# Streaming every second block backwards, and shifting where the weights lie in their slots

## The reference

```python
h = rms_norm(x, norm_g); proj = h @ w_in          # 2048 x 16512
...                                               # band attention, RWKV-7 scan, memory attention
merged = (sigmoid(ga) * (ya @ w_up_a) + sigmoid(gb) * (yb @ w_up_b) + sigmoid(gc) * (yc @ w_up_c))
x = x + merged @ w_o
...                                               # second layer: attention, gated linear attention, convolution
x = x + (silu(h2 @ w_ffn_gate) * (h2 @ w_ffn_up)) @ w_ffn_down
```

## Time and profile before

| | |
|---|---|
| median of 2 runs | 2914.97 us (2914.79 to 2915.15) |
| span of the profiled execution | 2913.4 us |
| PE busy | 2882.6 us, 99% |
| PE weight loads | 2491.1 us, 86%, beside the matmuls |
| DVE busy | 1619.3 us, 56% |
| ACT busy | 1344.1 us, 46% |
| HBM traffic | 177 GB/s over the span |

### The profile page before, as it was taken

How to read it: one execution, slowest core, us unless ns; L and a number is a source line. 1 busy time by engine, 2 the same in 40 slices (tenths; PEclk the granted TensorE clock), 3 DMA queues, 4 the chain that set the end, 5 groups by cost and what they waited for, 6 DMA issues and landing times.

```text
span 2913.4 us, 42709 instructions
## 1 busy us (share of the span) xinstructions
PE 2882.6 (99%) x18228; PEld 2491.1 (86%) x18228; DVE 1619.3 (56%) x1860; ACT 1344.1 (46%) x1533; POOL 73.7 (3%) x173
## 2 busy tenths in 40 slices
PE   7999999999999999999999999999999999999998
PEld 7979888888988888889998899888888888888886
DVE  5565665656656556564555466554654544544444
ACT  5452543544554454454455454444444444444443
POOL 5000000001000000000000000000000000000000
PEclk9999999999999999999999999999999999999999
DMA  7443444566665655566556566666566666666564
GB/s 211 125 143 112 134 128 118 166 195 184 227 194 184 189 163 185 191 188 182 174 161 202 166 174 174 196 194 195 192 184 195 188 193 188 188 189 206 192 194 152
DMA packets 356178, 518.30 MB, mean 178 GB/s; under 512 B 18288, under 2 KB 137220, under 8 KB 355220
## 3 DMA queue, kind: packets, MB, share of 16 engines
q1 hardware_dynamic: 355220, 512.37, 58.7%
q0 software_dynamic: 768, 3.20, 0.4%
HBM read 513.39 MB, written 2.11 MB: 177 GB/s over the span
## 4 chain that ended last, share of the span: by engine, by line
PE 98%; DVE 1%; ACT 0%; DMA 0%; issue 0%; SPq 0%; DVEq 0%; ACTq 0%
PE gp L1668 23%; PE gp L1670 23%; PE gp L1669 23%; PE gp L1677 7%; PE gp L1679 7%; PE gp L1678 7%; PE ps L1845 4%; PE ps L1727 1%; PE ps L1802 1%; PE ps L1833 1%; DMA gain<-in_norm_g 0%; PE ps L1787 0%; PE ps L1823 0%; PE ps L2045 0%; PE ps L2062 0%; PE ps L2053 0%
## 5 line engine op out<-in xcount | busy, mean ns | idle before, releaser
L1058 DVE TENSOR_TENSOR w_lo<-w_raw,w_hi 128x1024 fp32r<-128x1024 f32 (+2 forms) x976 | 1166.2, 1202 | 949.6 <-ACT w_hi L653 944.7
L653 ACT ACTIVATE w_hi<-w_raw 128x1024 fp32r<-128x1024 f32 (+2 forms) x976 | 1011.0, 1041 | 1106.4 <-PE gp L1670 877.7
L1668 PE MATMUL gp<-w_hi,h_hi 128*128 128x512 f32 x2112 | 833.5, 395 | 1.5 <-DVE w_lo L1058 1.5
L1670 PE MATMUL gp<-w_lo,h_hi 128*128 128x512 f32 x2112 | 822.7, 390 | 0.0
L1669 PE MATMUL gp<-w_hi,h_lo 128*128 128x512 f32 x2112 | 822.2, 389 | 0.0
L1677 PE MATMUL gp<-h_hi,w_hi 128*128 128x256 f32 x1696 | 488.4, 288 | 1.8 <-DVE h_lo L1123 1.8
L1678 PE MATMUL gp<-h_lo,w_hi 128*128 128x256 f32 x1696 | 474.5, 280 | 0.0
L1679 PE MATMUL gp<-h_hi,w_lo 128*128 128x256 f32 x1696 | 474.3, 280 | 0.0
L1668 PEld LDWEIGHTS gp<-w_hi,h_hi 128*128 128x128 f32 x2112 | 396.6, 188 | 83.8 <-DVE w_lo L1058 1.9
L1670 PEld LDWEIGHTS gp<-w_lo,h_hi 128*128 128x128 f32 x2112 | 396.5, 188 | 83.3
L1669 PEld LDWEIGHTS gp<-w_hi,h_lo 128*128 128x128 f32 x2112 | 396.8, 188 | 80.5 <-issue 0.5
(11 more groups left out here) (290 smaller groups left out, 1805.3 us busy)
## 6 DMA issues: line engine op xcount, KB each, us to landing
w_raw<-in_w_in SPq DMA_DIRECT2D x384, 512.0 KB, 4.0
w_raw<-in_w_ffn_gate SPq DMA_DIRECT2D x88, 512.0 KB, 4.4
w_raw<-in_w_ffn_up SPq DMA_DIRECT2D x88, 512.0 KB, 4.4
w_raw<-in_w_ffn_down SPq DMA_DIRECT2D x88, 512.0 KB, 4.1
w_raw<-in_w_in SPq DMA_DIRECT2D x136, 256.0 KB, 3.2
w_raw<-in_w_in SPq DMA_DIRECT2D x128, 192.0 KB, 3.1
w_raw<-in_w_mem_kv SPq DMA_DIRECT2D x32, 512.0 KB, 4.3
w_raw<-in_w_o SPq DMA_DIRECT2D x32, 512.0 KB, 4.3
```

Source lines behind the costliest of these rows:

```text
L653: act.activation(in_slot(w_hi, n), w_raw[:, slot, 0:size], ACT.Copy).then_inc(sem("hi_done"), 1)
L1058: dve.tensor_tensor(in_slot(w_lo, n), w_raw[:, slot, 0:size], in_slot(w_hi, n).bitcast(F32), ALU.subtract)\
L1668: pe.matmul(o, xh, wh, start=(k == 0), stop=False)
L1670: ins = pe.matmul(o, xh, wl, start=False, stop=(k == last_k))
```

## The change

The kind of block no longer decides alone where a unit lies. The blocks of each form are counted in pairs. Both of a pair get the same place in the slot: words 0, 63, 62, 61, 1, 2, 3 in turn for rows blocks, words 16, 0, 48, 32 for column blocks. The second of each pair is streamed backwards: its moving operand is read, and its PSUM output written, from the last column to the first. The sums are the same, column by column. The stationary operand is read forwards as before. Nothing else differs: instructions, their order, their waits and the DMAs are the same in number.

```diff
-SHIFT = {'rows': 0, 'wide': 16, 'pair': 16, 'trio': 16, 'narrow': 16}
+ROW_PLACES = (0, 63, 62, 61, 1, 2, 3)
+COLUMN_PLACES = (16, 0, 48, 32)
@@ build
+    place, back, of_form = [], [], Counter()
+    for b in blocks:
+        form = "rows" if b.kind == "rows" else "columns"
+        places = ROW_PLACES if form == "rows" else COLUMN_PLACES
+        place.append(places[of_form[form] // 2 % len(places)])
+        back.append(of_form[form] % 2 == 1)
+        of_form[form] += 1
...
+        def streamed(v, m):
+            return v[:, ::-1] if back[m] else v
...
         def in_slot(w, n):
-            at = SHIFT[blocks[units[n][0]].kind]
+            at = place[units[n][0]]
             return w[:, n % RING, at:at + unit_size(n)]
@@ PE's unit
-                        wh, wl = (in_slot(w, n)[:, j * 512:(j + 1) * 512] for w in (w_hi, w_lo))
+                        wh, wl = (streamed(in_slot(w, n)[:, j * 512:(j + 1) * 512], m) for w in (w_hi, w_lo))
...
-                            o = gp[:, s, a * 512:(a + 1) * 512]
+                            o = streamed(gp[:, s, a * 512:(a + 1) * 512], m)
...
-                        o = gp[:, s, c * T:(c + 1) * T]
+                        o = streamed(gp[:, s, c * T:(c + 1) * T], m)
+                        xh, xl = streamed(x_hi[k], m), streamed(x_lo[k], m)
...
-                        pe.matmul(o, wh, x_hi[k], start=(k == 0 and c % 2 == 0), stop=False, skip_group_check=True)
-                        pe.matmul(o, wh, x_lo[k], start=False, stop=False, skip_group_check=True)
-                        ins = pe.matmul(o, wl, x_hi[k], start=False, stop=(k == last_k), skip_group_check=True)
+                        pe.matmul(o, wh, xh, start=(k == 0 and c % 2 == 0), stop=False, skip_group_check=True)
+                        pe.matmul(o, wh, xl, start=False, stop=False, skip_group_check=True)
+                        ins = pe.matmul(o, wl, xh, start=False, stop=(k == last_k), skip_group_check=True)
```

## The result

The changed kernel takes 2983.72 us (median of 2 runs, 2982.74 to 2984.70) against 2914.97 us: 1.024 times as long, with a 95% interval from 1.021 to 1.027. The span of its profiled execution is 2983.0 us against 2913.4.

A forecast was written before the change was run, and what follows sets the result against it. PE's matmul pitches were taken to bound the kernel. 2913.4 + 3.2 (shifted start) + 0 + 0 gave a span of 2916.6 us; with 1.6 us between span and median, 2918 us; range 2844 to 3045 us.

The forecast's parts named there:

- rival 5: Address and direction don't touch PE's matmul pitch: 2915 us; chance 0.60, shared with the forecast itself.
- rival 3: Backward streams on PE pay one further cycle in 16 columns, 18 for 16: +71 us, 2989 us; chance 0.13.
- What bounds the kernel: PE, busy 2882.6 of 2913.4 us, hardly waits; the time is the sum of its matmuls' pitches.
- the counts: Rows blocks have 8928 matmuls, 7632 not at word 0, 4080 backwards; column blocks have 5088, 2544 backwards.
- The shifted start: Streamed weights of rows blocks starting off word 0: 0.42 ns a matmul, 3.2 us; ends 0 and 54 us.
- The backward stream: Reversed reading and PSUM writing in every second block on PE: taken as 0; ends -71 and +1223 us.
- POOL's row: POOL's reversed copy, 256 columns in 407 ns against 512 forward in 710, read as showing no backward penalty.
- Half rate backwards: Backward read or PSUM write on PE goes one column in two cycles: +1223 us, 4141 us; chance 0.17.
- Odd words straddle: Odd starts of PE's streams break every aligned pair of words fetched: +1132 us, about 4050 us; chance 0.03.
- The surplus goes in backward streams: PE's surplus cycle in 16 columns vanishes when streaming backwards: -71 us, 2847 us; chance 0.07.
- Column places: Stationary operand's words 16, 0, 48, 32 in column blocks: taken as 0; ends -13 and +9 us.
- Plain fp32: Score matmuls on PE read as 2.03 cycles a column without surplus, so the surplus belongs to fp32r operands.

## Why the prediction was right or wrong

The time, 2984 us, lies inside the range of 2844 to 3045 us, on the side "slower" that had a chance of 0.33; the likeliest value, 2918 us, which had 0.60 together with "nothing at all happens" (rival 5), was wrong by 66 us, and the result lies outside its own range of 2902 to 2973 us. That rival 3 came within 5 us, at 2989, is luck: it had 71 us from the direction and next to nothing from the places, where the direction alone cost 30.4 us and the places alone 47.3.

*What bounds the kernel* was right: PE's pitches alone carry the result, no wait of PE changed, and ACT and DVE stayed hidden. So were the counts, which turn the pitches into the 69 us. DVE's wait for ACT, which I had expected to stay near 945 us, rose to 1000.0, in step with PE's 70.4 us.

*The shifted start* is the step that failed first. I took 0.42 ns a matmul and 3.2 us in all; the places alone made the rows blocks 40.3 us longer, 5.3 ns for each of 7632 matmuls. The end of 54 us held, but I chose by DVE's two equal rows. DVE takes words at less than half the rate (1224 ns for 1024 of them against 0.443 ns each), and in plain fp32, at 429.2 ns a record, PE doesn't feel the address either. The row was near in form and says nothing of an fp32r stream. The surplus in the earlier trace rows had pointed the right way, and I used it only for the size of the smallest step.

*The backward stream* was taken at 0; alone it made the rows blocks 26.1 us longer, 6.7 ns for a backward matmul in most blocks. Rival 3 had the mechanism's form (a further share of a cycle for 16 columns of a backward stream) at twice the size: half a cycle more, not one, at place 0, and the full one only at places 3 and 63. POOL's row had the same fault as DVE's.

*Half rate backwards* (rival 1) didn't come, and neither side of its argument was needed: PSUM takes a step of -1 at no cost, against the rule that the Trainium skill gives in PSUM — Partial Sum Buffer, Specifications, if -1 is read as non-contiguous. For SBUF, the Trainium skill (SBUF — State Buffer, Specifications) asks for two hits in a line of 16 bytes for full bandwidth, and says too that each crossing to a new line pays a penalty. A step of 2 makes two hits and took 451.3 ns, so here the measurement decides against the two hits. My reading of the same row, that a backward unit step with its four hits changes nothing, was wrong by 6.7 ns at the least. *Odd words straddle* (rival 2) is refuted by words 7, 15, 39 and 63. *The surplus goes in backward streams* (rival 4) fell: 233.3 ns, not 213.

*Column places* were taken at 0 with +9 us as the upper end, on the ground that place 16 alone shows both pitches. The places alone cost 4.6 us (6.9 without the first block), the whole change 10.8 us there, with lasting pitches of up to 120 ns that the trace of before doesn't have. That end was too low: two observed pitches are not a bound.

*Plain fp32* was misread: the four records of the earlier trace rows are two matmuls, not four, so that a column costs four cycles and not two. Nothing in the sum hung on it, but a "half rate" was named after it.

What stays open is the rule. Shown is that at place 0 the cost of the direction arises in reading the moving operand from SBUF, that neither it nor place 1 costs anything in plain fp32, that the stationary operand's address and length take part, and that a pitch once taken holds on until a new block or other work comes: within a stretch of 60 or more matmuls of one block, the mean of 24 pitches moves by more than 1 ns in none of eleven traces. That the places cost by the same reading is argued: the shift alters nothing else of PE, and the pitch doesn't follow ACT's and DVE's work. What order of accesses makes 0, 7, 15, 39 and 63 free and 1, 5 and 17 dear was not found. That the places 61, 60 or 5 have two pitches each, in blocks of the same form, says that how the two streams begin relative to each other matters as well; this is argued, not shown.

## What to carry to other kernels

Where an engine's stream has a small surplus over its nominal rate, it may stand at a limit, and then address, step and direction of its operand are no longer free; evidence from an engine that runs at a lower rate, or from another format, can't be carried over to it. Measure pitches between starts, not durations, and let neighbouring blocks of one program carry the variants: one trace then compares them all. A place that is best for one form of block can also set the pitch of the next form, so sweep it on the whole program.

## What the runs showed of the hardware that was not expected

- fp32r matmuls of 512 columns: 226.7 ns at best from a moving address, 216.7 ns from one word read again and again, 451.3 ns with every second word.
- One operand's place in steps of 4 bytes moves the pitch between 226.7 and 240 ns; word 16 of a slot costs 2.3 ns, words 7, 15 and 63 nothing.
- Streaming backwards costs 6.7 to 13.3 ns a matmul of 512 columns; at place 0 all of it is in the reading, and writing PSUM backwards costs nothing.
- A shorter weight load can slow the stream: 231.6 ns with 32 columns where 128 gave 226.8.
- A plain fp32 matmul of 512 columns is two records and costs 858 ns, at place 0, at place 1 and backwards.
- Column blocks have lasting pitches of 113.3, 117.7 and 120.0 ns, and which one they take can hang on the block before (113.3 behind words 7, 15 and 63, 117.8 behind 0 and 1).
